# Paired attentions: the probabilities scaled on GpSimd, the transposed probabilities copied by VectorE and ScalarE, one bank each

## The reference

```
s = q @ k.T * scale + mask            # or + bias
p = exp(s - max(s)) / sum(exp(s - max(s)))
o = p @ v                             # the sparse attention: times a gate of the token and the head
```

## Time and profile before

| | |
|---|---|
| median of 3 runs | 2275.18 us (2274.31 to 2277.2) |
| profiled execution, its own time | 2273.97 us |
| its span | 2272.1 us |
| TensorE busy / VectorE / ScalarE | 98% / 79% / 51% of the span |
| mean granted clock of TensorE | 0.994 |
| nsa0, moba0, nsa1, na0 lie at | 93 to 146, 425 to 454, 1026 to 1079, 1991 to 2046 us |

### The profile page before, as it was taken

One profiled execution on the slowest core, in us unless ns is written; L12 is line 12 of the kernel. 1 busy time (PEld: TensorE's weight loads), 2 busy tenths in 40 slices (PEclk: granted clock), 3 DMA queues, 4 the chain that ended last, 5 costly groups with the idle time before them and its releaser, 6 DMA issues.

```text
span 2272.1 us, 37955 instructions
## 1 busy us (share of the span) xinstructions
PE 2217.3 (98%) x15228; PEld 1975.1 (87%) x15228; DVE 1786.1 (79%) x3510; ACT 1163.2 (51%) x2054; POOL 0.2 (0%) x4
## 2 busy tenths in 40 slices
PE   7999999999999999999999999999999999999998
PEld 7878889898889988896988987788888889979998
DVE  7788977789887898878898865577877876478888
ACT  4685554665553555458655634534122235476433
POOL 0000000000000000000000000000000000000000
PEclk9999999999999999999999999999999999999999
DMA  7326666356665565660665532023554523434563
GB/s 246 136 71 219 234 195 219 121 190 235 199 211 186 197 235 198 214 209 23 210 235 198 181 121 75 1 75 123 175 180 163 176 75 103 140 103 149 204 227 126
DMA packets 70159, 373.58 MB, mean 164 GB/s; under 512 B 7392, under 2 KB 16736, under 8 KB 37984
## 3 DMA queue, kind: packets, MB, share of 16 engines
q1 hardware_dynamic: 61472, 361.52, 46.6%
q10 hardware_dynamic: 8512, 9.63, 1.4%
HBM read 369.03 MB, written 1.05 MB: 163 GB/s over the span
## 4 chain that ended last, share of the span: by engine, by line
PE 81%; DVE 10%; ACT 4%; DMA 3%; issue 1%; ACTq 0%; DVEq 0%
PE ps L482 79%; DVE w_lo L1778 3%; DMA w_raw<-weights 3%; DVE hid_f L2183 1%; DVE hid_f L2168 1%; ACT w_hi L1171 1%; PE ps L745 1%; ACT hid_f L1371 1%; PE ps L806 1%; DMA sm<-small 1%; PE ps L735 1%; PE ps L789 0%; ACT hid_f L1384 0%; DVE v_sb L2282 0%; DVE a_both L1778 0%
## 5 line engine op out<-in xcount | busy, mean ns | idle before, releaser
L482 PE MATMUL ps<-a_both,w_hi 128*128 128x256 f32 (+1 forms) x4864 | 1187.5, 330 | 17.8 <-DVE a_both L1835 10.5
L482 PEld LDWEIGHTS ps<-a_both,w_hi 128*128 128x128 f32 x4864 | 808.2, 190 | 95.9 <-issue 16.2
L482 PE MATMUL ps<-a_both,w_lo 128*128 128x256 f32 (+1 forms) x3136 | 886.2, 291 | 0.0
L1778 DVE TENSOR_TENSOR w_lo<-w_raw,w_hi 128x1024 fp32r<-128x1024 f32 (+1 forms) x632 | 708.0, 1148 | 89.5 <-ACT w_hi L1171 82.2
L482 PEld LDWEIGHTS ps<-a_both,w_lo 128*128 128x128 f32 x3136 | 595.3, 190 | 26.4
L1171 ACT CAST w_hi<-w_raw 128x1024 fp32r<-128x1024 f32 (+1 forms) x448 | 414.8, 975 | 381.1 <-DMA w_raw<-weights 380.3
L482 PE MATMUL ps<-hid_both,w_hi 128*128 128x512 f32 (+2 forms) x2216 | 600.2, 350 | 6.2 <-DVE hid_both L1778 2.3
L482 PEld LDWEIGHTS ps<-hid_both,w_hi 128*128 128x128 f32 x2216 | 385.7, 189 | 64.2 <-issue 4.6
L482 PE MATMUL ps<-hid_both,w_lo 128*128 128x256 f32 (+2 forms) x1460 | 438.1, 304 | 0.0
L482 PEld LDWEIGHTS ps<-hid_both,w_lo 128*128 128x128 f32 x1460 | 276.4, 189 | 14.3
L1177 ACT CAST w_hi<-w_raw 128x1024 fp32r<-128x1024 f32 (+2 forms) x184 | 187.7, 1020 | 1.3 <-DMA w_raw<-weights 1.2
(11 more groups left out here) (235 smaller groups left out, 1920.0 us busy)
## 6 DMA issues: line engine op xcount, KB each, us to landing
w_raw<-weights SPq DMA_DIRECT2D x250, 1024.0 KB, 4.8
pe_sb<-weights SPq DMA_DIRECT2D x96, 512.0 KB, 5.6
w_raw<-weights SPq DMA_DIRECT2D x64, 704.0 KB, 4.0
pe_sb<-na_bias ACTq DMA_DIRECT2D x32, 128.0 KB, 2.2
X<-x_t SPq DMA_DIRECT2D x2, 512.0 KB, 7.0
X<-c_rows ACTq DMA_DIRECT2D x2, 512.0 KB, 4.1
qk<-qk ACTq DMA_DIRECT2D x4, 256.0 KB, 6.8
qk<-ctx_t ACTq DMA_DIRECT2D x1, 1024.0 KB, 5.6
```

The lines of the kernel that those rows point to most:

```text
L482: return nc.tensor.matmul(out, stationary, moving, start=start, stop=stop)
L1778: return v.tensor_tensor(out, a, b.bitcast(F32), ALU.subtract)
```

## The change

`normalize` on VectorE becomes `factors`: the reciprocal and the gate product alone, which now raise a new semaphore `factors`. A new program on GpSimd waits for it and does the scalings, item by item, in the four paired attentions; it raises `p_ready`. The copy of the transposed probabilities is cut by bank: ScalarE copies the bank of the first 64 query rows, VectorE, one step later in its order, that of the others; each raises `t_taken`, and TensorE waits for both.

```diff
--- before.py
+++ after.py
@@ -222,7 +222,7 @@
         hid_f, hid_h, hid_ready = sem("hid_f"), sem("hid_h"), sem("hid_ready")
         low_copied, gate_scaled, silu_done = sem("low_copied"), sem("gate_scaled"), sem("silu_done")
         dve_step, act_step = sem("dve_step"), sem("act_step")
-        att = {n: {e: sem(f"{n}_{e}") for e in ("s_ready", "s_taken", "exp_done", "p_ready", "t_ready",
+        att = {n: {e: sem(f"{n}_{e}") for e in ("s_ready", "s_taken", "exp_done", "factors", "p_ready", "t_ready",
                                                 "t_taken", "pv_done", "o_hi", "o_ready")}
                for n in ("nsa0", "nsa1", "moba0", "mla0", "na0")}
         nsa_once = {e: sem(e) for e in ("gelu_t", "gates_copied", "gates_t", "gates", "cmp_scores", "cmp_shifted", "cmp_exp", "cmp_p", "cmp_t")}
@@ -385,6 +385,11 @@
             w = 2 * WIDTH[name]
             at = 0 if name == "na0" else FT * S - PAIR_SLOTS * w
             return hid_f32[1][:, at + i % PAIR_SLOTS * w:at + (i % PAIR_SLOTS + 1) * w]
+
+        def turned(name, i, r):
+
+            tokens = t_pair(name, i).rearrange("p (n r c) -> p r n c", r=2, c=HD)[:, r]
+            return tokens, ps[:, PAIR_T[r], 0:WIDTH[name]].rearrange("p (n c) -> p n c", c=HD)
 
         NEG_SCALE = {"nsa0": -HD ** -0.5, "nsa1": -HD ** -0.5, "moba0": -HD ** -0.5,
                      "mla0": -float(np.float32((NOPE + ROPE) ** -0.5)), "na0": -1.0}
@@ -783,7 +788,7 @@
                     b = i - 2
                     if 0 <= b < N:
                         pe.wait_ge(a["p_ready"], b + 1)
-                        wait(pe, a["t_taken"], b)
+                        wait(pe, a["t_taken"], 2 * b)
                         for at in range(0, 2 * W, P):
                             for r in range(2):
                                 last = nc.tensor.transpose(ps[:, PAIR_T[r], at // 2:at // 2 + HD], p_pair(name, b)[half(r), at:at + P],
@@ -795,7 +800,7 @@
                     if 0 <= b < N:
                         it = items[b]
                         o = PAIR_O[it["tile"] % 2]
-                        pe.wait_ge(a["t_taken"], b + 1)
+                        pe.wait_ge(a["t_taken"], 2 * b + 2)
                         if it["tile"] >= 2:
                             pe.wait_ge(a["o_ready"], it["tile"] - 1)
                         many = len(it["heads"][0]["pv"])
@@ -1380,8 +1385,7 @@
                         act.wait_ge(a["t_ready"], b + 1)
                         if b >= PAIR_SLOTS:
                             act.wait_ge(a["pv_done"], b - PAIR_SLOTS + 1)
-                        turned = ps[:, PAIR_T[0]:PAIR_T[1] + 1, 0:W].rearrange("p r (n c) -> p r n c", c=HD)
-                        nc.scalar.copy(t_pair(name, b).rearrange("p (n r c) -> p r n c", r=2, c=HD), turned).then_inc(a["t_taken"], 1)
+                        nc.scalar.copy(*turned(name, b, 0)).then_inc(a["t_taken"], 1)
                     if behind:
                         behind(i)
                     b = i - 3
@@ -1760,6 +1764,26 @@
                 run[stage_name](arg)
 
 
+        @block.gpsimd
+        def _(pool):
+
+            def pair_attention(name):
+
+                a, items = att[name], ITEMS[name]
+                W = WIDTH[name]
+                for b, it in enumerate(items):
+                    pool.wait_ge(a["factors"], b + 1)
+                    for e in range(2):
+                        for r, (c, _) in enumerate(it["rows"]):
+                            at = p_pair(name, b)[:, e * W + c.start:e * W + c.stop]
+                            x = len(it["rows"]) * e + r
+                            last = nc.gpsimd.tensor_scalar(at, at, recip[:, b % 4, x:x + 1], None, ALU.mult)
+                    last.then_inc(a["p_ready"], 1)
+
+            for name in ("nsa0", "moba0", "nsa1", "na0"):
+                pair_attention(name)
+
+
         @block.vector
         def _(dve):
             cnt = Counts()
@@ -2150,23 +2174,17 @@
                 a, items = att[name], ITEMS[name]
                 N, W = len(items), WIDTH[name]
                 tiles = 0
-                def normalize(b):
-                    rows = items[b]["rows"]
-                    w = 2 * len(rows)
+                def factors(b):
+                    w = 2 * len(items[b]["rows"])
                     g = items[b]["gate"]
                     dve.wait_ge(a["exp_done"], b + 1)
-                    step(v.reciprocal(recip[:, b % 4, 0:w], sums[:, b % 4, 0:w]))
+                    last = v.reciprocal(recip[:, b % 4, 0:w], sums[:, b % 4, 0:w])
                     if g is not None:
+                        step(last)
                         sync()
                         both = recip[:, b % 4, :].rearrange("p (e r) -> p e r", e=2)
-                        step(v.tensor_tensor(both, both, gate[:, :, g:g + REP + 1:REP].rearrange("p r e -> p e r"), ALU.mult))
-                    sync()
-                    for e in range(2):
-                        for r, (c, _) in enumerate(rows):
-                            at = p_pair(name, b)[:, e * W + c.start:e * W + c.stop]
-                            x = len(rows) * e + r
-                            last = v.tensor_scalar(at, at, recip[:, b % 4, x:x + 1], None, ALU.mult)
-                    last.then_inc(a["p_ready"], 1)
+                        last = v.tensor_tensor(both, both, gate[:, :, g:g + REP + 1:REP].rearrange("p r e -> p e r"), ALU.mult)
+                    last.then_inc(a["factors"], 1)
 
                 for i in range(N + 4):
                     if i < N:
@@ -2185,11 +2203,17 @@
                                                               ALU.add, ALU.min, negmax[:, i % 4, x:x + 1])
                         last.then_inc(a["s_taken"], 1)
                     if 0 <= i - 1 < N and i != 2:
-                        normalize(i - 1)
+                        factors(i - 1)
                     if i == 1:
-                        normalize(1)
+                        factors(1)
                     if beside:
                         beside(i)
+                    b = i - 2
+                    if 0 <= b < N:
+                        dve.wait_ge(a["t_ready"], b + 1)
+                        if b >= PAIR_SLOTS:
+                            dve.wait_ge(a["pv_done"], b - PAIR_SLOTS + 1)
+                        v.tensor_copy(*turned(name, b, 1)).then_inc(a["t_taken"], 1)
                     b = i - 4
                     if 0 <= b and items[b]["last"]:
                         tiles += 1
```

## The result

| | kernel before | kernel after |
|---|---|---|
| median of 4 runs, us | 2274.74 | 2343.77 (2337.43 to 2347.18) |
| ratio, 95% interval | | 1.0297 (1.0285 to 1.0309) |
| profiled execution: time, span, us | 2273.97, 2272.1 | 2337.43, 2335.6 |
| end of nsa0, moba0, nsa1, na0 in the trace, us | 147.11, 455.58, 1080.13, 2047.01 | 165.15, 479.30, 1125.23, 2110.99 |

The change makes the kernel 3.0% slower; the forecast was 2279, its range ended at 2296. The end of a stage is the start of VectorE's first instruction behind it. These ends say where the 64 us arise: 18.0 in nsa0, 5.7 in moba0, 21.4 in nsa1 and 18.9 in na0, and nothing between the stages (64 us is the difference of the two profiled executions; by the medians it is 69). All of it is in the four paired attentions, even in na0, where the forecast saw no loss.

A forecast was written before the change was run, and what follows sets the result against it. The round through ScalarE's copy, 3.48 + G, replaces full engines as bound. Steady +1.0 and +0.3, fill +1.6, drain +1.2: +4.1 us, 2279; range 2271 to 2284, or 2265 to 2296 over both ends of G.

The forecast's parts named there:

- a second round goes through TensorE's queue and spans three items: 5.83 + G: In nsa0, transposes, values, scores, shift, exponentials, factors and scaling; 5.16 us for two items at G = 1.91, not binding.
- G: Time from the factors to the transposes, with GpSimd's scaling and hand-over: 1.91 us taken, 1.11 low, 2.69 high.
- break-even: In nsa0, the G of 1.83 us at which the round through ScalarE's copy equals the 5.31 of before.
- The full engines: In nsa0 before, VectorE (busy 5.16) and ScalarE (5.31) were said to set the 5.31 us of two items.
- GpSimd is dear: Rival: GpSimd's scaling becomes the longest step of the round; about +21 us, 2296, at G = 2.69; chance 0.20.
- the prediction's own round: In nsa0, exponentials, factors, scaling, transposes, ScalarE's copy, half the cast: 3.48 + G, 5.39 us for two items.
- na0: "nothing": In na0 the round of 4.82 us stays under TensorE's 5.04 for two items, so the steady part changes by 0.
- Fill +0.4 and drain +0.3 a stage: Scaling exposed at each stage's start and end: +0.4 and +0.3 us in each of four, +1.6 and +1.2 in all.
- The half that was to come back from an earlier shift: At each stage's start, an earlier shift of the next item gives back about half of +0.85 us, leaving +0.4.
- The clock: Rival: longer TensorE idle slows the next values in the other stages, +1 us each; chance 0.08 together with the collision.
- The collision at the drain: Rival: at stage ends GpSimd's scaling and VectorE's subtraction exclude each other; +3 to +5 us, 2283; 0.08 with the clock.
- TensorE could be reached at two items of 4.7 to 4.8: Quick rival: at G 1.2 or less, nsa0 falls to TensorE's 4.70 for two items; about -9.5 us, 2266; chance 0.25.

The follow-up runs named there:

- two wide products: Changed kernel with one product of two tensors per block for both heads, factor broadcast, two GpSimd instructions in place of four: 2290.13 us in one run.
- the one-head run: Changed kernel with GpSimd scaling only the first head of each item in all four attentions, the second left unscaled: 2282.99 us in one run.
- 5: Changed kernel with VectorE issuing the factors of item i-1 ahead of the shift of item i: 2322.17 us in one run.
- experiment 10: Changed kernel with TensorE issuing the next item's scores ahead of the values, the values one item later: 2319.16 us, ratio 1.0179.
- Experiment 7: Kernel before with transposes, copies and values one item later in nsa and moba, four probability slots for three: 2278.82 us, ratio 1.0012.
- experiment 8: Kernel before with GpSimd scaling one 128x128 block of four in nsa and moba, VectorE the other three: 2274.37 against 2276.04 us, ratio 0.9997.

## Why the prediction was wrong

The four cells that tell the causes apart, as median time and two items of nsa0:

| | values ahead of scores | scores ahead of values |
|---|---|---|
| VectorE scales (1.01) | 2274.74; 5.31 | 2274.18; 5.21 |
| GpSimd, two wide products (1.61) | 2290.13; 5.96 | 2274.82; 5.29 |
| GpSimd, four scalings (2.98) | 2343.77; 7.34 | 2319.16; 6.67 |

- **The step that failed first: "a second round goes through TensorE's queue and spans three items: 5.83 + G".** It led the round from the shift over the exponentials of the same item to its factors, and so took three items. The shorter way is through VectorE's queue: the factors of item k+2 stand behind the shift of k+3, whatever the exponentials do. That round spans two items and is 4.31 + G. The prediction named the queue ("behind it stand the cast's low part and the next shift") and did not ask what stands behind the shift. Its break-even is thus not G = 1.83 but 1.06, the time that VectorE took: the kernel before had no slack at all for a slower scaling. Shown by the one-head run and the wide products, which are slower at G = 1.55 and 1.66, and by the two orders changed (5, 10), each of which shortens the two items.
- **The bound of before was misread with it.** The full engines seemed to explain 5.31, with the gaps between VectorE's instructions as its own. Experiment 7 gives them 5.16; the 5.31 is the round. Two bounds 0.15 apart look alike in a busy share, the more so as a wait of 0.12 lay hidden in ScalarE's.
- **The second step: G.** 1.91 was taken, bounds 1.11 and 2.69; it is 3.03 in nsa and moba (2.98 + 0.05) and 3.16 in na0 (forecast 1.55), above the upper bound. The rows of ScalarE bound nothing for GpSimd. "GpSimd is dear" was the rival that came true, and went further than its own price. Of the 1.95 us between the forecast 5.39 and the measured 7.34 for two items, 1.12 is the price put into the prediction's own round (3.48 + 3.03 = 6.51) and 0.83 the round that it missed. (0.15 of these 0.83 the prediction's own round would have made as well, had it counted the whole cast of 0.26 in place of half.)
- **na0: "nothing".** There the same round is 4.16 + 3.16 = 7.32 against TensorE's 5.04; it makes 18.9 us.
- **Fill +0.4 and drain +0.3 a stage.** The third transposes of nsa0, the exposed ones of the earlier trace rows, start at 109.50 in place of 107.47, +2.0, for the forecast's +0.4; from the fourteenth transposes to the end of the stage another 3.3 are lost. The half that was to come back from an earlier shift did not.
- **The clock**, a rival at +1 a stage, cost more where it came. Two items of nsa0 over which TensorE's clock fell, then two of nsa1 before and two after it fell:

```profile
127.91:136.54 8.63, 6.24 (x60) 4.24 (x61) 4.37 (x23) 4.84 (x19) 5.96 (x9) 0.80 0.01 3
...
1075.46:1082.59 7.13, 4.92 (x60) 3.22 (x61) 4.15 (x24) 4.56 (x19) 5.93 (x8) 1.00 0.00 0
...
1090.62:1099.34 8.72, 6.43 (x63) 4.35 (x60) 4.62 (x23) 4.84 (x19) 5.94 (x8) 0.75 0.00 1
```

  After the windows in which TensorE was busy 4.9 of 7.1 to 7.3 us, the granted clock of nsa1's window is 0.75 in the mean, between its levels of 2.4 and 1.2 GHz. Values and scores are links of the round, so it grows with them, to 8.72. Five pairs of nsa1 take 41.5 us in place of 5 x 7.34 = 36.7, and one of nsa0 8.63: 6 us of the 64. With the wide products, at two items in 5.96, the clock stays at 0.99 and 1.00 in both stages. In experiment 10 it is 1.00 in each pair from 112.37 to 139.06, with TensorE busy 4.63 of 6.67. What made the clock fall where it did is not settled by these runs.
- **The collision at the drain**, a rival at +3 to +5 in all, came as well. At the end of each stage VectorE splits weights while GpSimd scales. In nsa0:

```profile
154.86 3.71 POOL L1780 TENSOR_SCALAR hid_f<-hid_f,recip 128x128 f32<-128x128 f32 x4 [0.73 <-DVE recip L2186]
...
156.42 1.36 DVE L1802 TENSOR_TENSOR w_lo<-w_raw,w_hi 128x1024 fp32r<-128x1024 f32 x1
```

  The four take 3.71 in place of 2.98, and all of the 0.73 falls on the fourth. It starts at 156.92, when the subtraction still has 0.86 to run, and takes 1.65 in place of 0.92. The third, already running when the subtraction starts, keeps its 0.60; there the subtraction loses 0.14 (1.36 in place of the 1.22 of the earlier trace rows). In na0 GpSimd's last scaling starts just behind the subtraction and takes 2.55 in place of 1.56:

```profile
2101.74 1.22 DVE L1802 TENSOR_TENSOR w_lo<-w_raw,w_hi 128x1024 fp32r<-128x1024 f32 x1
...
2101.84 2.55 POOL L1780 TENSOR_SCALAR hid_f<-hid_f,recip 128x512 f32<-128x512 f32 x1
```

  With 0.86 in moba0 and 0.73 in nsa1 that is 3.3 us, and in each stage the last transposes wait for it. The Trainium skill ("SBUF — State Buffer", "Who interferes with whom") says that VectorE with two SBUF inputs contends with a GpSimd instruction that reads SBUF and, of VectorE's 2-port modes, that whoever issues first gets the shared pair for the whole instruction while the other fully blocks. Where VectorE came first the trace nearly agrees: GpSimd loses 0.98 of the 1.12 us that both run in na0. Where GpSimd came first it doesn't: VectorE loses 0.14 in 0.52 of overlap.
- **What was right.** The new copies (0.48 on ScalarE, 0.56 on VectorE, forecast 0.48 and 0.55), the busy times of both engines, the round through ScalarE's copy (but for the cast), and that TensorE could be reached at two items of 4.7 to 4.8, if only with every round opened.

## What to carry to other kernels

Before work is handed to a slower engine, close every round through the queues of all engines, and at each step ask not only what data an instruction needs but what stands ahead of it in its queue: here a 0.4 us instruction without open inputs tied the scaling to TensorE's order. If the links of such a round add up to the measured period, then that round is the bound, even where two engines look full, and each nanosecond added to a link is paid. An engine that has never run such an instruction in the trace has no bound from its neighbours: one short run of it is worth more than any range, and so is a try of its other forms.

## What the runs showed that was not expected

- On GpSimd, an in-place float32 product with a scalar of each partition costs 2.5 ns an element (602, 922 and 1564 ns for 128, 256 and 512, undisturbed), and with a constant 2.5 as well (528 and 848 for 128 and 256). A product of two tensors, the second broadcast, costs 1.67 (613, 1039 and 1893 ns for 256, 512 and 1024). The form with two tensor operands is the cheaper one by a third. Why is not settled by these runs.
- The Trainium skill ("GPSIMD Engine Reference", "Elementwise — side-by-side cycle accounting") has about 1.8 cycles an element at 1.2 GHz for a tight loop with one input and 2.6 for two inputs. At that rate the measured 2.5 and 1.67 ns would be 3.0 and 2.0 cycles (an estimate), in the opposite order; the measurement decides.
- A GpSimd scaling that starts while VectorE's subtraction of two SBUF operands runs stands for nearly all that is left of it: 0.73 of 0.86, 0.98 of 1.12 us. One that VectorE's subtraction meets already running keeps its length. With both engines scaling (experiment 8), GpSimd's 602 ns become 748, and VectorE's 348 become 459 to 466 for the block that starts under GpSimd's.
- ScalarE, recorded as busy in 5.31 of 5.31 us, waited 0.12 of them: the next instruction can start 0.09 after a readout of 0.2 us, so the record of the readout covers a wait of that size.
